# Narrower waits for index scores and the first attention pair, and later turns of finished rows, in a two-block transformer kernel

## The chip, the core and the metric

The kernel runs on one core of one Trainium2 chip. The metric is the device time of one execution in microseconds. The change is judged by the medians of several runs of each kernel. TensorE (PE) multiplies matrices and turns (transposes) tiles into PSUM, VectorE (DVE) and ScalarE (ACT) read PSUM and write SBUF, GpSimd (POOL) and SyncE (SP) issue DMAs. Each engine works through its own list in order and waits on semaphores.

## The reference

Two blocks of two layers each work on 512 rows of width 1024, all in float32.

```python
# first block, each layer
h = x @ w_in                     # split in diff_q/k/v, dsa_q/k/v, idx_q/k/w, fox_q/k/v/f, gate
a  = rms(diff_attention(rope(dq), rope(dk), dv, lam)) * g_subln     # 4 heads
bo = dsa_attention(...)          # keys chosen by index scores, top 128
co = forgetting_attention(...)   # 4 heads
x  = layer_norm(ALPHA * x + (concat(a, bo, co) * silu(gate)) @ w_out)
# the choice of keys in dsa_attention
sc = einsum('bqhd,bsd->bqhs', qi, ki)
idx_score = einsum('bqhs,bqh->bqs', relu(sc), wi)
_, idx = top_k(where(causal, idx_score, -inf), topk)

# second block, each layer (256 context rows beside the 512)
q, k, v = split(modulate(rmsnorm(x)) @ w_qkv)    # 16 query heads, 4 key heads of 64
o = window_attention(...)        # layer 0, with a sink per head
o = global_attention(...)        # layer 1, with normed queries and keys
x = x + gate_a * (o @ w_o)
x = x + gate_f * moe(modulate(rmsnorm(x)))       # 32 experts, 2 for each row
return rmsnorm(x)
```

## The kernel before

`make_plan` writes out one list of steps, and every engine walks through the same list in `build`, each doing its share of a step. The order of the steps is therefore the order of each engine's work. Rows are in tiles of 128 (`t`). Three rings carry the work between the engines: the two banks of `PJ` (projections and weighed values), the two banks of `TR` (turned tiles), the two halves of `SC` (scores). A use number counts up for each ring (`n["tr"]` for TR). TensorE waits before use k of TR until use k-2 was copied out (`tr_slot`, `tr_free`), and ScalarE copies each turned bank to SBUF and then adds one to `tr_free`.

First block. For each chunk of w_in (`idx_q`, `idx_k`, `dsa`, `fox`, `diff_q`, `diff_k`, `diff_v`, `gate0`, `gate1`) and each tile there is a `project` step (L1120 to L1129), then `flush(1)`, which issues the `stage_turn` (L1136) of the tile before: TensorE turns what VectorE rotated into STG, and ScalarE copies it to QK. In the three chunks dsa, fox and diff_q (`ci` 2, 3, 4) an `index` step follows (L1155): scores of one pair of index heads for the query tile `ci - 1`, which ScalarE passes through relu and VectorE weighs and sums. Further `topk` steps of VectorE go through the summed scores. TensorE waits in an index step until `tr_free` has reached `s.tr_before`, the number of all TR uses planned up to there. The step reads blocks 8 to 11 (idx_q) and 12 (idx_k) of QK alone. In the first dsa tile a `forget` step stands between the turn and the index step.

Second block. The columns of w_qkv come in three chunks c in the order 0, 2, 1 (queries of heads 0 to 7, keys and values, queries of heads 8 to 15), with a `qkv` step (L1288) per tile and a `qk_turn` (L1302) of the tile before by `flush2(1)`. Attention runs in units, one head of one query tile each, two units per call of `attend_pair(unit_list, i, after)`. A call issues the scores of units i and i+1, the turn of i-2 (L1186), the exponential of i, the weighing of i-3 (L1196), the exponential of i+1, the turn of i-1 and the weighing of i-2. ScalarE copies each turn into PT. The first call stands before the last `qkv` step of chunk 1. Its first unit waits for `tr_free` to reach `u.needs`, again all uses planned so far. It reads keys and queries of head 0 of tile 0. In layer 1 VectorE and ScalarE do their part of that last `qkv` step only in the step `qkv_late`, after pair 2. `flush2(0)` turns this late tile after pair 4. `rq`, in layer 1, also after pair 4, takes roots and reciprocals of the query norms for heads 8 to 15. `gains`, in layer 0, after pair 8, folds gains into the rope tables on VectorE.

When the last unit k of a query tile has been weighed, VectorE divides the result into O2, and `after[k]` issues the `o_turn` step: TensorE waits for `pj_free`, turns the 1024 columns of the tile in two banks (`turn_rows`, L1081), and ScalarE copies both to XT. `attend_pair` issues it at the end of pair k+3. There are six such tiles in layer 0 (80 units) and four in layer 1 (64 units). The output projection (`wo_first`, `wo`, L1086) follows after all pairs.

Of the kernel before, what the change touches and what calls it, by code (L numbers as in the profile page):

```python
# [171 lines left out]
def make_plan(until=99):  # L172


    steps = []
    n = dict(pj=0, tr=0, sc=0, stg=0, unit=0, fin=0, bc=0, topk=0, idx=0, ada=0, mixed=0, part=0, sinks=0, routed=0)
# [3 lines left out]
    def take(what, k=1):  # L180
        n[what] += k
        return list(range(n[what] - k, n[what]))
# [14 lines left out]
    def add(kind, **kw):  # L197
        s = Step(kind=kind, tr_before=n["tr"] - len(kw.get("tr", ())), **kw)
        steps.append(s)
        users = kw.get("w")  # L200
        if users is not None and kw.get("last", True):

            for u, use in zip(users if isinstance(users, list) else [users], kw["pj"] if isinstance(kw["pj"], list) else [kw["pj"]]):
                u.done = use + 1
        return s

    def begin_unit(u, first):
        u.sc = take("sc")[0]
        u.index = attend.count
        attend.count += 1  # L210
        u.two_before = units_before[-2] if len(units_before) >= 2 else None
        units_before.append(u)
        n["mixed"] += u.kind == "diff"
        u.mixed = n["mixed"]
        u.first = first
        if u.slot == 0:
            attend.batch += 1
            n["sinks"] += u.kind in ("window", "ctx")
        u.batch, u.sinks = attend.batch, n["sinks"]
        s = add("scores", u=u)  # L220
        u.needs = s.tr_before

    def turn_unit(u):
        u.tr = take("tr", -(-u.blocks // 4))
        add("turn", u=u)
# [10 lines left out]
    def attend_pair(unit_list, i, after):  # L236


        m = len(unit_list)
        if i < m:  # L240
            begin_unit(unit_list[i], i == 0)
            begin_unit(unit_list[i + 1], False)
        if 2 <= i < m + 2:
            turn_unit(unit_list[i - 2])
        if i < m:
            add("exp", u=unit_list[i])
        if 4 <= i:
            weigh_unit(unit_list[i - 3])
        if i < m:
            add("exp", u=unit_list[i + 1])  # L250
        if 2 <= i < m + 2:
            turn_unit(unit_list[i - 1])
            weigh_unit(unit_list[i - 2])
        if i - 3 in after:
            after[i - 3]()

    def attend(unit_list, extra=None, after=None):

# [37 lines left out]
    for l in range(DEPTH):  # L296
# [29 lines left out]
        for ci, name in enumerate(names):  # L326
            w = weight("w_in", l=l, cols=CHUNKS[name])
            for t in range(XT_TILES):
                if l and ci == 0 and t == XT_TILES - 1:
                    xt_ready[t] = add("fin_turn", f=fins[t], tr=take("tr", 2)).tr[-1]  # L330
                s = project(name, t, w)
                turn_staged(s)
                flush(1)
                if name == "dsa" and t == 0:
                    add("forget", l=l, pj=take("pj")[0])
                if ci >= 2:

                    if ci - 1 in (1, 2, 3):
                        add("index", l=l, t=ci - 1, h=2 * t, sc=take("sc")[0], index=take("idx")[0])
                    for tt in (1, 2, 3):  # L340
                        if topk_left[tt] and tt < ci - 1:
                            k = min(4 if ci < 5 else 2, topk_left[tt])
                            topk_left[tt] -= k
                            add("topk", l=l, t=tt, rounds=k, last=topk_left[tt] == 0,
                                count=n["topk"] + (topk_left[tt] == 0))
                            n["topk"] += topk_left[tt] == 0
                            break
            if name == "idx_k":
                add("log_f", l=l)
# [6 lines left out]
        unit_list = []  # L356
# [47 lines left out]
    for l in range(DEPTH):  # L404
# [5 lines left out]
        def flush2(keep):  # L410
            while len(prev) > keep:
                add("qk_turn", s=(s := prev.pop(0)), tr=take("tr", s.turns))

        unit_list, last_unit = [], []
# [15 lines left out]
        def oturn(t):  # L430
            def go():
                turned[t] = add("o_turn", t=t, after=unit_list[last_unit[t]].pj, tr=take("tr", 2)).tr[-1]
            return go

        after = {k: oturn(t) for t, k in enumerate(last_unit)}
        late = None
        for p, c in enumerate((0, 2, 1)):
            w = weight("w_qkv", l=l, c=c)
            ts = list(range(XT_TILES) if (last and c < 2) else range(tiles))
            if l == 0 and c == 0:  # L440
                ts = ts[XT_TILES:] + ts[:XT_TILES]
            if l and c == 2:
                add("load2", l=l)
                add("layer2", l=l)
                add("rq", l=l, c=0)
            for t in ts:
                if p == 2 and t == ts[-1]:
                    attend_pair(unit_list, 0, after)
                if l == 0 and c == 0 and t == 0:
                    xt_ready[XT_TILES - 1] = add("fin_turn", f=fins[-1], tr=take("tr", 2)).tr[-1]  # L450
                two = c < 2 and t < XT_TILES
                ahead = combines[4 * p + t + 1] if l and 4 * p + t + 1 < len(combines) else None
                tr = take("tr", 2) if ahead else None
                s = add("qkv", l=l, c=c, t=t, w=w, last=t == ts[-1], pj=take("pj")[0], stg=take("stg", 2 if two else 1),
                        turns=2 if two else 1, inner=(ahead, tr) if ahead else None)
                if l and p == 2 and t == ts[-1]:
                    late = s
                    s.late = True
                s.ready = xt_ready[t] if (l == 0 and c == 0) or (l and (c == 0 or (c == 2 and t >= XT_TILES))) else None
                if ahead:  # L460
                    xt_ready[ahead.t] = tr[-1]
                prev.append(s)
                if l and 4 * p + t + 2 < len(combines):
                    add("combine_end", f=combines[4 * p + t + 2], l=l - 1)
                    if 4 * p + t + 3 < len(combines):
                        front(4 * p + t + 3)
                flush2(1)
        for i in range(2, len(unit_list) + 4, 2):
            attend_pair(unit_list, i, after)
            if i == 2 and late:  # L470
                add("qkv_late", s=late)
            if i == 4:
                if l:
                    add("rq", l=l, c=1)
                flush2(0)
            if i == 8 and l == 0:
                add("gains", l=l)
# [23 lines left out]
        t = moe_tiles - 1  # L501
# [2356 lines left out]
```

How the kernel before makes its waits and increments, by code:

```python
        def w_ready(eng, u):  # L971
            eng.wait_ge(w_loaded[u.slot], 16 * (u.loads))
# [9 lines left out]
        @block.sync  # L982
# [2 lines left out]
            def free(prev):  # L985
                if prev is not None:
                    sp.wait_ge(sc_full if units[prev].kind in ("gate", "up") else pj_full, units[prev].done)
# [26 lines left out]
            n = 0  # L1015
            while n < len(units):
                u = units[n]
                if u.kind not in ("gate", "up", "down"):
                    load_unit(u)
                    n += 1
                    continue
                m = units[n:n + 3 * EXPERTS]
                base, l = n, u.l
                sp.wait_ge(pj_full, attended[l])
                for k in range(8):
                    free(m[k].prev)
                    load_expert(m[k], m[k].e)
                with sp.Fori(0, 14) as i:
                    for k in range(8, 14):
                        sp.wait_ge(pj_full if m[k].kind == "down" else sc_full,
                                   i * (4 if m[k].kind == "down" else 2) + m[k - 6].done)
                        load_expert(m[k], i * 2 + m[k].e)
                for k in range(92, 96):
# [4 lines left out]
                    for u in units[n:n + 3]:  # L1039
                        load_unit(u)
                    n += 3
                o = over[l]
                sp.wait_ge(over_ready, l + 1)
                sp.wait_ge(pj_full, m[-1].done)
                count = sp.value_load(OVI[0:1, MAX_OVER:MAX_OVER + 1], min_val=0, max_val=MAX_OVER)
```

## Time and profile before

| | us |
|---|---|
| runs, median of 3 | 2954.38 (2951.1 to 2954.95) |
| profiled execution, whole | 2950.66 |
| its span in the profile | 2949.0 |
| TensorE busy | 2803.7 (95%) |
| VectorE busy | 1144.1 (39%) |
| ScalarE busy | 761.1 (26%) |
| GpSimd busy | 323.3 (11%) |

The span goes roughly as follows: projections of the first layer to 285 us, its attention to 400, the second layer of the first block from 460 to 850 with the same stages, projections of the second block to 1070, window attention to 1243, experts from about 1360 to 1940, the last layer's projections to 2080, its attention to 2253, experts again to the end. Times in a timeline are microseconds from the span's start. A row of it gives start and duration of one or more merged instructions, the engine, the line of the kernel, the operation with its tiles and shape, and their number. A bracket gives the idle time of the engine ahead of it and who ended that. All VectorE and ScalarE work is recorded under L140. A matmul of float32 counts as several instructions.

### The profile page before, as it was taken

Reading aid. Unit: us, or ns where it says so; the run is one execution under the profiler, and the core shown is the slowest. Engines: PE = TensorE matmul, PEld = TensorE weight load, DVE = VectorE, ACT = ScalarE, POOL = GpSimd, SP = SyncE. Lnnn points to the kernel's source line nnn. Section 1 sums busy time; section 2 is a strip of 40 time slices with the busy share of each in tenths; the row PEclk is TensorE's granted clock in tenths of the full one; section 3 lists DMA queues with packets and bytes.
Section 4 is the critical chain, followed back from the end, with each engine's and each line's share of the span. In section 5 each row is a group of like instructions: output and inputs, shape, how many; then the busy total and the mean of one; then the engine's idle time right before and its main releaser. Section 6 shows DMA issues by size and latency. Waiting matters only on the chain. (4 is left out here: it accounts for less than half of the span.)

```text
span 2949.0 us, 65190 instructions
## 1 busy us (share of the span) xinstructions
PE 2803.7 (95%) x27105; PEld 1659.6 (56%) x27109; DVE 1144.1 (39%) x2781; ACT 761.1 (26%) x1599; POOL 323.3 (11%) x584
## 2 busy tenths in 40 slices
PE   8999999999889999999999999989899999999996
PEld 4444655444554457645666666644576566666663
DVE  2572653472654245545211122253443611112214
ACT  1111531110542147621111111143674111111111
POOL 3000430000440000011010000020000100000011
PEclk9999999999989999999999999999999999999998
DMA  7212653211653100146999999962002599999994
GB/s 272 70 57 86 231 161 97 78 66 57 238 186 137 57 1 2 57 166 222 397 401 400 397 398 401 396 235 99 1 2 108 210 384 400 399 399 401 399 400 169
DMA packets 155504, 636.94 MB, mean 216 GB/s; under 512 B 19744, under 2 KB 24352, under 8 KB 138960
## 3 DMA queue, kind: packets, MB, share of 16 engines
q1 hardware_dynamic: 114624, 517.59, 45.5%
q0 software_dynamic: 40720, 117.18, 11.7%
q8 instruction: 106, 1.74, 0.2%
q14 instruction: 54, 0.44, 0.0%
HBM read 582.70 MB, written 52.00 MB: 215 GB/s over the span
## 5 line engine op out<-in xcount | busy, mean ns | idle before, releaser
L1128 PE MATMUL PJ<-WR,XT 128*128 128x512 f32 (+2 forms) x1152 | 475.2, 568 | 5.7 <-ACT XT L140 2.9
L140 ACT ACTIVATE PT<-TR 128x512 f32<-128x512 f32 (+3 forms) x384 | 177.8, 493 | 880.6 <-PE TR L1357 736.9
L1128 PEld LDWEIGHTS PJ<-WR,XT 128*128 128x128 f32 x1152 | 215.6, 191 | 243.9 <-issue 215.7
L140 DVE TENSOR_TENSOR PR<-G 128x384 f32<-128x384 f32 x64 | 35.8, 559 | 737.9 <-ACT G L140 737.5
L1086 PE MATMUL PJ<-WR,XT 128*128 128x512 f32 x576 | 260.1, 608 | 1.8 <-ACT XT L140 1.4
L1337 PE MATMUL SC<-QK,XT 128*64 128x256 f32 x2112 | 244.1, 385 | 0.0
L140 DVE TENSOR_REDUCE SM<-SC 128x1 f32<-128x768 f32 (+6 forms) x208 | 173.7, 835 | 152.6 <-PE SC L1106 143.8
L1288 PE MATMUL PJ<-WR,XT 128*128 128x512 f32 x512 | 227.1, 596 | 1.0 <-issue 1.0
L1337 PE MATMUL SC<-WR,XT 128*64 128x256 f32 x1984 | 226.2, 381 | 0.0
L1337 PEld LDWEIGHTS SC<-QK,XT 128*64 128x64 f32 x2112 | 150.2, 138 | 86.3 <-issue 16.0
L140 ACT ACTIVATE PR<-SC,SM 128x256 f32<-128x256 f32 (+5 forms) x288 | 187.6, 669 | 41.4 <-DVE SM L140 27.2
L140 ACT ACTIVATE XT<-TR 128x384 f32<-128x384 f32 (+1 forms) x204 | 99.6, 526 | 343.8 <-PE TR L1323 241.6
L1086 PEld LDWEIGHTS PJ<-WR,XT 128*128 128x128 f32 x576 | 110.2, 195 | 133.5 <-issue 131.3
L1337 PEld LDWEIGHTS SC<-WR,XT 128*64 128x64 f32 x1984 | 139.8, 137 | 79.6 <-issue 12.3
L1196 PE MATMUL PJ<-V,PT 128*64 128x65 f32 (+1 forms) x3904 | 169.0, 233 | 1.4 <-ACT PT L140 1.4
L1106 PE MATMUL SC<-QK 64*128 64x512 f32 (+7 forms) x512 | 157.5, 522 | 10.8 <-ACT PR L140 10.6
L1186 PE MATMUL TR<-KF,PR 128*128 128x128 f32 x976 | 149.2, 282 | 10.0 <-DVE PR L140 7.4
L1196 PEld LDWEIGHTS PJ<-V,PT 128*64 128x64 f32 x3904 | 136.8, 138 | 36.4 <-issue 33.4
L1288 PEld LDWEIGHTS PJ<-WR,XT 128*128 128x128 f32 x512 | 95.2, 191 | 109.1 <-issue 109.1
L140 ACT ACTIVATE QK<-TR 128x512 f32<-128x512 f32 (+4 forms) x108 | 59.2, 563 | 369.7 <-PE TR L1136 272.6
L2765 POOL DMA_DIRECT2D y_rows<-XT x62 | 33.2, 535 | 950.1 <-DVE XT L140 925.2
L1347 PE MATMUL SC<-QK,XT 128*32 128x128 f32 x4224 | 127.9, 273 | 0.0
(253 smaller groups left out, 3344.0 us busy)
## 6 DMA issues: line engine op xcount, KB each, us to landing
QK<-in_w_gate_dram SPq DMA_DIRECT2D x34, 2048.0 KB, 9.5
WR<-in_w_down_dram SPq DMA_DIRECT2D x34, 2048.0 KB, 15.8
QK<-in_w_up_dram SPq DMA_DIRECT2D x32, 2048.0 KB, 14.4
WR<-in_w_up_dram SPq DMA_DIRECT2D x32, 2048.0 KB, 14.4
WR<-in_w_gate_dram SPq DMA_DIRECT2D x30, 2048.0 KB, 9.5
QK<-in_w_down_dram SPq DMA_DIRECT2D x30, 2048.0 KB, 15.9
WR<-in_w_ada_dram SPq DMA_DIRECT2D x24, 2048.0 KB, 8.1
WR<-in_w_in_dram SPq DMA_DIRECT2D x14, 2048.0 KB, 7.9
```

What stands on the lines that cost most here:

```text
L140: return lambda *a, **k: Signal(make(*a, **k), self)
L1086: m = mm(dst[:, 0:n], rows[:, c, :], w[:, c, 0:n], start=c == 0, stop=c == DC - 1)
L1106: m = mm(SC[:, u.sc % 2, col:col + n], lhsT, rhs, start=all(p[0] // 512 != bank for p in ps[:k]), stop=all(p[0] // 512 != bank for p in ps ...
L1128: m = mm(bank[:, 0:n], XT1[:, c, s.t * P:(s.t + 1) * P], w[:, c, 0:n], start=c == 0, stop=c == DC - 1)
L1186: m = turn(bank[:, b * P:(b + 1) * P], src, identF)
L1196: m = mm(bank[r:r + HALF_ROWS, col:col + n], PT[:, o + r:o + r + HALF_ROWS], v, start=b == 0, stop=b == len(vs) - 1)
L1288: m = mm(bank, rows[:, c, :], w[:, c, :], start=c == 0, stop=c == DC - 1)
L1337: mm(bank[CAP_A * h:CAP_A * (h + 1), k * 512:k * 512 + 256], XET[par][:, c, 0:CAP_A], w[:, c, 256 * h:256 * (h + 1)], start=c == 0, stop=c ...
L1347: x = mm(bank[CAP_B * q:CAP_B * (q + 1), k * 512 + 256:k * 512 + 384], XET[par][:, c, CAP_A:CAP], w[:, c, P * q:P * (q + 1)], start=c == 0 ...
L2765: dma(dst, YR[r % 2][0:CAP]).then_inc(y_stored[r % 2], 16)
```

## The change

In `attend_pair` the call of `after` moves: from the end of pair k+3 to the middle of pair k+5, between the exponential of unit i and the weighing of unit i-3. The weighing of i-3 gets an upper bound, since the loop now runs one pair further (the last pair holds only the last `o_turn`). In the first block the index steps get `indices_turned` as the value that they wait for, taken at the first dsa tile ahead of the first index step. In the second block the first unit gets `keys_turned`, taken after the turns behind the first tile of chunk 1. `flush2(0)` moves from pair 4 to pair 8, in both layers, and stands before `gains` in layer 0; `rq` stays.

```diff
@@ attend_pair
         if i < m:
             add("exp", u=unit_list[i])
-        if 4 <= i:
+        if i - 5 in after:
+            after[i - 5]()
+        if 4 <= i < m + 4:
             weigh_unit(unit_list[i - 3])
         if i < m:
             add("exp", u=unit_list[i + 1])
         if 2 <= i < m + 2:
             turn_unit(unit_list[i - 1])
             weigh_unit(unit_list[i - 2])
-        if i - 3 in after:
-            after[i - 3]()
@@ make_plan, first block
                 if ci >= 2:
 
+                    if ci == 2 and t == 0:
+                        indices_turned = n["tr"]
                     if ci - 1 in (1, 2, 3):
                         add("index", l=l, t=ci - 1, h=2 * t, sc=take("sc")[0], index=take("idx")[0])
+                        steps[-1].tr_before = indices_turned
@@ make_plan, second block
                 if p == 2 and t == ts[-1]:
                     attend_pair(unit_list, 0, after)
+                    unit_list[0].needs = keys_turned
@@
                 flush2(1)
-        for i in range(2, len(unit_list) + 4, 2):
+                if p == 2 and t == ts[0]:
+                    keys_turned = n["tr"]
+        for i in range(2, len(unit_list) + 6, 2):
             attend_pair(unit_list, i, after)
             if i == 2 and late:
                 add("qkv_late", s=late)
             if i == 4:
                 if l:
                     add("rq", l=l, c=1)
+            if i == 8:
                 flush2(0)
             if i == 8 and l == 0:
                 add("gains", l=l)
```

## Rows read from the trace of the kernel before

**Rows 1.** The page's busy times: engine, busy us (share of the span), instructions.

```profile
PE 2803.7 (95%) x27105; PEld 1659.6 (56%) x27109; DVE 1144.1 (39%) x2781; ACT 761.1 (26%) x1599; POOL 323.3 (11%) x584
```

**Rows 2.** TensorE's waits: line, releaser: us in total, times, longest.

```profile
PE TR L1081 <- DVE G L140: 25.3, 15, 5.2
PE SC L1155 <- ACT QK L140: 17.5, 22, 1.0
```

**Rows 3.** TensorE's timeline, turn and index in a dsa, a fox, a diff_q step.

```profile
82.60 0.49 PE L1136 MATMUL TR<-KF,STG 128*128 128x128 f32 x3
83.75 0.70 PE L1155 MATMUL SC<-QK 64*128 64x256 f32 x4 [0.66 <-ACT QK L140]
...
114.43 1.04 PE L1136 MATMUL TR<-KF,STG 128*66 128x128 f32 x8
116.41 0.92 PE L1155 MATMUL SC<-QK 64*128 64x384 f32 x4 [0.95 <-ACT QK L140]
...
172.66 0.60 PE L1136 MATMUL TR<-KF,STG 128*128 128x128 f32 x4
174.03 1.13 PE L1155 MATMUL SC<-QK 64*128 64x512 f32 x4 [0.77 <-ACT QK L140]
```

**Rows 4.** TensorE's timeline, a turn and scores that don't wait, layer 1, second block.

```profile
2079.13 1.04 PE L1302 MATMUL TR<-KF,STG 128*128 128x128 f32 x8
2080.10 0.48 PE L1106 MATMUL SC<-V,QK 64*128 64x256 f32 x1
```

**Rows 5.** Stretches: us, busy PE, PEld, DVE, ACT, POOL; clock, DMA share, GB/s.

```profile
83.75:106.61 22.86, 20.87 (x70) 10.95 (x70) 9.73 (x38) 3.26 (x6) 0.00 (x0) 1.00 0.27 92
145.83:183.00 37.17, 34.86 (x98) 15.38 (x99) 31.53 (x71) 6.11 (x8) 0.00 (x0) 1.00 0.16 57
1400.00:1600.00 200.00, 200.00 (x2829) 126.75 (x2823) 42.85 (x83) 23.73 (x55) 19.25 (x35) 1.00 1.01 399
```

**Rows 6.** VectorE's timeline, the index sum in a diff_q step.

```profile
176.41 1.54 DVE L140 SCALAR_TENSOR_TENSOR BC<-PT,SM,BC 128x512 f32<-128x512 f32 x2 [0.68 <-ACT PT L140]
```

**Rows 7.** TensorE's timeline, turn and first pair's scores, layers 0 and 1.

```profile
1059.66 1.04 PE L1302 MATMUL TR<-KF,STG 128*128 128x128 f32 x8
1061.51 0.48 PE L1106 MATMUL SC<-V,QK 64*128 64x256 f32 x1 [0.82 <-ACT QK L140]
...
2067.26 1.04 PE L1302 MATMUL TR<-KF,STG 128*128 128x128 f32 x8
2070.67 0.48 PE L1106 MATMUL SC<-V,QK 64*128 64x256 f32 x1 [2.37 <-ACT QK L140]
```

**Rows 8.** Timelines of TensorE and ScalarE around the first `o_turn` of layer 0.

```profile
1105.41 0.80 PE L1196 MATMUL PJ<-V,PT 128*64 128x65 f32 x20
1107.37 1.06 PE L1081 MATMUL TR<-KF,G 128*128 128x128 f32 x8 [1.16 <-ACT PT L140]
1108.36 0.48 PE L1106 MATMUL SC<-V,QK 64*128 64x256 f32 x1
...
1106.63 0.77 ACT L140 ACTIVATE PT<-TR 128x512 f32<-128x512 f32 x2
```

**Rows 9.** Timelines of TensorE, ScalarE, VectorE around layer 1's late turn.

```profile
2089.03 0.92 PE L1196 MATMUL PJ<-V,PT 128*64 128x65 f32 x24
2094.68 1.94 PE L1302 MATMUL TR<-KF,STG 128*128 128x128 f32 x8 [4.73 <-ACT PT L140]
...
2109.17 0.48 PE L1106 MATMUL SC<-V,QK 64*128 64x256 f32 x1
...
2092.92 0.99 ACT L140 ACTIVATE PR<-SC,SM 128x768 f32<-128x768 f32 x1 [0.28 <-DVE SM L140]
2094.88 1.28 ACT L140 ACT_TABLE_LOAD   x1
...
2096.91 0.18 DVE L140 TENSOR_SCALAR SM<-SM 128x32 f32<-128x32 f32 x1
```

**Rows 10.** The stretch behind the late turn, columns as in Rows 5.

```profile
2092.00:2102.00 10.00, 7.32 (x52) 5.44 (x52) 3.84 (x10) 6.66 (x11) 0.00 (x0) 0.66 0.00 0
```

## The prediction

> **What bounds the kernel now.** I read the page's busy times first: TensorE is busy for 95% of the span [rows 1]. A microsecond is won where TensorE stands still and nothing else takes the place of the wait, and nowhere else. So the second view is the list of what TensorE waited for, and in it two of the largest entries: 25.3 us of transposes (L1081) behind VectorE's G, and 17.5 us of index scores (L1155) behind ScalarE's QK, 22 waits [rows 2]. The source splits the first: L1081 is shared by every transpose of whole rows, and much of the 25.3 belongs to steps that the change leaves alone (its longest, 5.2 us, stands behind the sub-norm). The second is touched by the change in full. The rest is read instruction by instruction in the timeline of TensorE, ScalarE and VectorE around each touched place, always as start against start, since the "idle" of a row leaves out the tail of a matmul whose end is modelled.
>
> **Index scores.** The wait of `index` on `tr_free` asks for all turns so far, and so for the copy of the turn issued just ahead of it. With the new value it asks only for the turns of idx_q and idx_k, which were over before the first index step. Per layer there are 12 index steps; the first is already covered by `forget`, 11 wait. What stands between turn and index now, start to start: 1.15 us behind a turn of three blocks, 1.98 behind one of eight, 1.37 behind one of four [rows 3]. What would stand there without a wait: a turn of eight with scores of 64 rows behind it that don't wait takes 0.97 [rows 4]; eight blocks last 1.04 and four 0.60 [rows 3], 0.11 for each block, so 0.53 for four and 0.42 for three. The gain is then 0.73, 1.01 and 0.84 each. Per layer four follow a three-block turn (dsa, and the first fox step), four an eight-block turn (three fox steps and the first diff_q step), three a four-block turn: 2.9 + 4.0 + 2.5 = 9.5, twice 18.9 us. The lower end is the idle time that the waits show, 17.5 [rows 2]; the upper end counts no 0.1 for the change from 128 to 64 rows, 22 x 0.1 more, 21.1.
>
> Who would be late next? Behind the index stands the next projection, which needs a PJ bank that VectorE freed a period ago. ScalarE's relu comes after the copy in its order, and that copy is done by then or shortly after. VectorE is the engine to look at: in the diff_q steps it does the rotation, the index sum and four rounds of top-k, and is busy 31.53 of 37.17 us [rows 5]. In a step of 9.4 us (165 to 174) it stands idle for 0.68 only, behind the relu [rows 6], so it needs 8.7 us where TensorE would want 8.56. It falls behind by 0.15 us per step for three steps, and TensorE's turn of a staged tile comes a whole projection after VectorE wrote it, some six microseconds of slack. In the dsa steps it is busy for 9.73 of 22.86 [rows 5]. After diff_q two rounds stand in place of four and it catches up. I charge nothing.
>
> **First pair of the second block's attention.** Its scores now ask for all turns so far; with `needs` set after the last key turn they ask for nothing that is late. Layer 0: from turn to scores 1.85 us [rows 7], 0.97 without a wait, gain 0.9. Layer 1: 3.41 [rows 7], gain 2.4, since there the copy stands behind the staging copy and the square of the next tile on ScalarE. The exponentials of that pair come no earlier (VectorE takes their minima after its rotation), but TensorE has a projection before it needs them, and the next turn starts only at 2079.13 [rows 4]. In layer 1 ScalarE would end the second exponential just as the next turn is ready, so this cover is thin; without it up to 1 us goes. Sum 3.3, from 2.3 to 3.5.
>
> **Finished rows turned a pair later.** Ten `o_turn` steps; the last of each layer stays behind the last weighing, eight move. Before: the weighing starts at 1105.41 and lasts 0.80, the turn waits 1.16, the next scores start at 1108.36 [rows 8], so the step costs 2.15. The wait is for ScalarE: its copy of the preceding turn, at 1106.63, stands behind the pair's second exponential [rows 8]. Moved between `exp` and `weigh` of the following pair, the turn comes right behind the turn of unit i-2. Its rows have long been written by VectorE. The bank it needs is freed by a copy that ScalarE can start at once: bank full after 0.6, copy 0.6 (the pair of copies lasts 0.77 for five blocks [rows 8]), where TensorE would be there after 0.55, so it waits 0.7; with its own 0.9 that is 1.6. Queued behind it now are a weighing and the turn of unit i-1; its two copies, about 1.1 us (an estimate from 0.77 for five blocks), stand on ScalarE ahead of the pair's second exponential, and the turn of i-1 waits perhaps 0.1 for a bank. The pair after finds both exponentials done. Where a unit has four blocks one bank is already free and the wait is 0.4, but before it was shorter too. I take 2.15 + 0.1 - 1.6 = 0.7 for each, 5.6 for eight. Ends: nothing gained (each new wait as long as the old), and 8 x 1.2 = 9.6 with no wait left.
>
> **The late query tile.** Layer 1: the weighing at 2089.03 is done at 2089.9, and the turn of the late tile waits 4.73 us for a bank whose copy stands behind the exponential of unit 5; it starts at 2094.68 [rows 9]. The granted clock is 0.66 over the ten microseconds from 2092 [rows 10], so 6.8 of them at 1.2 GHz, and the turn lasts 1.94 instead of 1.04. The scores of pair 10 (units 10 and 11) start at 2109.17 [rows 9]. Without the turn there, the next scores wait for the two exponentials (unit 5's ends at 2093.91 [rows 9]) and start at about 2092.7. This wait of 2.8 us takes the place of the 4.8. Then comes the root of the query norms: its table load at 2094.88 takes 1.28 [rows 9], VectorE is held until 2097.1 [rows 9], takes the minima of units 6 and 7, and the exponentials, 0.99 each [rows 9], follow another table load, so that they end at about 2100.5 and 2101.5. Pair 8 then starts at about 2100.6, when the first of them has freed its scores, and takes 4.9, pair 10 without more would start at 2105.5. The late turn is now behind pair 8, in the position that `o_turn` leaves, and costs about 2.0 there: 2107.5 against 2109.17, gain 1.7. Should the clock fall here as well, the waits for VectorE absorb most of it (0.3). Ends: -1 (the root's chain a little later than I have it) and +5. Layer 0: the turn finds its bank free in both places; one pair before the `gains` step it covers some 0.5 us of waits behind it. Sum 2.2.
>
> The Trainium skill, "ScalarE: Activation LUTs", section "Table sets: the hidden batching unit", says to batch activations by set and prices a switch at about 2.7 us. That speaks against leaving the root between exponentials; by its price two loads would set pair 8 back by 2.8 us and the late tile would cost 1.1 instead of giving 1.7. The rows show 1.28 for a load in this kernel, and the measured value decides.
>
> **Sum.** 18.9 + 3.3 + 5.6 + 2.2 = 30.0 us. No instruction is added or removed, no DMA is moved, and the queues of SP and POOL keep their order.
>
> **Rivals.**
> (a) The moved turns give nothing, because ScalarE, loaded with two more copies inside a pair, makes the second exponential late: only the first two parts remain, 22.2. For it: two exponentials of 0.99 and two units' copies of at least 0.77 [rows 8, 9] keep ScalarE for over 3.5 us of a pair of some 4.9 already. Against it: the pair that follows has slack. 2928.5 by the profiled run.
> (b) The index waits turn into waits for VectorE or a bank and only the other parts count, 11.1: 2939.6. For it: the 0.68 us in [rows 6]. Against it: it concerns three steps a layer, and the lag is far from TensorE's need.
> (c) The gain is given back in the expert stage, whose DMA share is 1.01 from 1400 to 1600 [rows 5]: if the stream of weights began at a fixed time, TensorE would only wait for it, and the total would be unchanged, 2950.7. Against it: SP's loads wait for the last weighing and for consumed slots, so they move with TensorE.
> (d) Slower. The turns inside a pair leave short waits in a row (bank, weighing, bank) at eight places, and the clock falls to 1.2 GHz at each for 6.8 us as at 2092 [rows 10], which costs 3.4 us. With waits that long the moved turns give nothing either, so the base is that of (a): ten falls (eight turns, the two late tiles) are 34 against 22.2, 2962.5. [...]
> The Trainium skill, "TensorE: Matmul & The Clock Gate", section "A second HAM failure mode: psum-queue depth-cycling", says that frequent micro-idles between groups of matmuls make the clock oscillate. By that rule (d) is what eight new micro-idles do; the stretches of index steps, with one such idle each period, don't show it.
>
> **How the numbers follow.** The profiled execution took 2950.7 us (span 2949.0); less 30.0 that is 2920.7. The median of the runs before is 2954.4, 3.7 higher, and the profiled one lies below all three, so I add half of that: 2922.5. Chances: my forecast 0.82, (a) 0.08, (b) 0.05, (c) 0.03, (d) 0.02. The ends of the unknown parts: 17.5 + 2.3 + 0 - 1 = 18.8 and 21.1 + 3.5 + 9.6 + 5.5 = 39.7, which gives 2911 to 2932 by the profiled run; with the 3.7 of the median at the upper end, and (a) inside, 2911 to 2935. Of this kernel a measurement can tell about 0.2%, 6 us. Faster by more: forecast, (a) and (b), with a little off for what I didn't see, 0.94; within 0.2%: 0.04; slower: 0.02.
>
> **What would show it.** Right: no L1155 row with a wait in TensorE's list, index scores about 0.5 us behind a four-block turn and about 1.0 behind eight; first scores of the pairs 1.0 us behind their turn; `o_turn` inside a pair with a wait of 0.4 to 0.7 behind ScalarE's PT; layer 1's late turn behind pair 8, and between 2085 and 2105 no single wait over 3 us. Wrong: waits of a projection or a staged turn behind VectorE in the diff_q steps, scores waiting for the second exponential behind each `o_turn`, or new stretches of a granted clock of 0.5.

## The result, and the profile after

The changed kernel took 2923.79 us in the median (2922.1 to 2926.34, 4 runs), the kernel before 2952.74 beside it on the same chip (2945.94 to 2954.95, 4 runs). The ratio is 0.9906, with an interval of 0.989 to 0.9922: 29 us, or 0.94%, faster. The profiled execution took 2925.03 us with a span of 2923.3, so against the profiled one of before the span is 25.7 us shorter. The forecast was a median of 2922.5 us, and 30.0 us less than before in the profiled execution. The time was met, but the sum was 3 to 4 us higher than what the traces show. The parts below show where.

The page of the changed kernel, its busy times, and then TensorE's list of waits (line, releaser: us in total, times, longest). All lines of the helpers have moved down by 7: the index scores are L1162, the turns of whole rows L1088, the scores of a pair L1113, the late turn L1309.

```profile
PE 2798.9 (96%) x27109; PEld 1659.0 (57%) x27109; DVE 1143.9 (39%) x2781; ACT 760.9 (26%) x1599; POOL 323.9 (11%) x584
```

```profile
PE TR L1088 <- DVE G L140: 24.2, 14, 5.2
PE SC L1113 <- ACT PR L140: 15.5, 10, 2.7
...
PE TR L1088 <- ACT PT L140: 4.4, 8, 0.8
...
PE SC L1103 <- ACT XT L1740: 3.6, 1, 3.6
...
PE TR L1309 <- ACT PT L140: 1.1, 1, 1.1
```

Against [rows 1] the work is the same; what changed is idle time. The index scores (17.5 us in [rows 2]) have left the list. The 25.3 us behind VectorE's G have become 24.2, so that entry had, as supposed, little to do with the change. The scores behind ScalarE's PR have grown from 11.5 us in 9 waits to 15.5 in 10. The same entry in the list of before:

```profile
PE SC L1106 <- ACT PR L140: 11.5, 9, 2.5
```

It grew in layer 1, where waits of 2.74 and 1.28 us took the place of the late turn's 4.7; they are shown with the last experiment.

**Index scores.** TensorE's timeline of the changed kernel in the same diff_q step as in [rows 3]:

```profile
159.72 6.17 PE L1135 MATMUL PJ<-WR,XT 128*128 128x512 f32 x14
165.72 0.60 PE L1143 MATMUL TR<-KF,STG 128*128 128x128 f32 x4
166.25 1.13 PE L1162 MATMUL SC<-QK 64*128 64x512 f32 x4
167.31 1.13 PE L1135 MATMUL PJ<-WR,XT 128*128 128x512 f32 x2
```

Turn to scores is 0.53 us here, 1.37 in [rows 3]. From the first index step to the last a layer takes 87.79 us (78.46 to 166.25) where it took 97.32 (76.71 to 174.03), in both layers: 9.53 each, 19.06 together. Nothing turned up behind it: no projection or turn waits for VectorE in these stretches.

**The whole span, as a running account.** The same instruction is looked up in both traces, and the difference of its starts shows what has been won up to there.

| up to | before | after | won so far | part |
|---|---|---|---|---|
| first index step, layer 0 | 76.71 | 78.46 | -1.75 | start-up |
| last index step, layer 0 | 174.03 | 166.25 | 7.78 | index 9.53 |
| last index step, layer 1 | 624.00 | 606.34 | 17.66 | index 9.53 |
| output stage of layer 1 | 946.96 | 928.62 | 18.34 | small waits |
| weighing behind the first pair | 1072.72 | 1053.49 | 19.23 | first pair 0.89 |
| turn of unit 18 | 1103.27 | 1083.63 | 19.64 | late tile 0.41 |
| last row turn, layer 0 | 1243.50 | 1221.94 | 21.56 | five moved turns 1.92 |
| second block, layer 1, before its first pair | | | 22.42 | select, experts |
| behind that pair | 2084.73 | 2059.87 | 24.86 | first pair 2.4 |
| pair 10, layer 1 | 2109.17 | 2083.51 | 25.66 | late tile 0.80 |
| last row turn, layer 1 | 2252.87 | 2226.12 | 26.75 | three moved turns 1.09 |
| end of the span | 2949.0 | 2923.3 | 25.7 | experts |

So the change gave 19.06 + 3.3 + 3.0 + 1.2 = 26.6 us in these two executions. The start-up cost 1.75, and the stretches that the change doesn't touch moved both ways, by up to 1.6 us at one place (the wait of L1103 in the list above is 3.6 us here and 2.0 in the same place before). Such stretches vary from trace to trace. From the last row turn of layer 1 to the end of the span, where no edit lies, five traces take 694.7 to 697.2 us (before and changed among them) and the seven others 700.7 to 701.5, and a second trace of the changed kernel is one of those. The medians of the kernel before differ in the same way from chip to chip, 2948.84 to 2954.26 us. A part of a few microseconds is therefore read inside its own stretch and not from the whole span.

### The profile page after: what moved, and what is told of

It is laid out like the page before. It is cut to its first block and busy times, and to the rows that moved or that the text cites. A ratio compares the mean times of both kernels' runs of the same rounds, so it can differ in the third digit from the quotient of the medians.

```text
span 2923.3 us, 65195 instructions
## 1 busy us (share of the span) xinstructions
PE 2798.9 (96%) x27109; PEld 1659.0 (57%) x27109; DVE 1143.9 (39%) x2781; ACT 760.9 (26%) x1599; POOL 323.9 (11%) x584
## 5 line engine op out<-in xcount | busy, mean ns | idle before, releaser
L1113 PE MATMUL SC<-QK 64*128 64x512 f32 (+7 forms) x512 | 157.7, 522 | 11.1 <-ACT PR L140 11.0
```

Source lines behind the costliest of these rows:

```text
L1113: m = mm(SC[:, u.sc % 2, col:col + n], lhsT, rhs, start=all(p[0] // 512 != bank for p in ps[:k]), stop=all(p[0] // 512 != bank for p in ps ...
```

## The experiments

Each is one kernel, read in the same way; where several executions were timed, the median, the range and the ratio to the kernel before on the same chip stand with it.

### The index scores alone

```diff
 (kernel before)
+                    if ci == 2 and t == 0:
+                        indices_turned = n["tr"]
 ...
+                        steps[-1].tr_before = indices_turned
```

> The kernel before with nothing but the index steps' new value for their wait. My theory: the index waits alone carry 19 of the gain, since TensorE bounds the projection steps and nothing is late behind them: about 19 us faster than before (0.64%), first to last index step 9.5 us shorter in each layer, and no wait of a projection or a staged turn behind VectorE. Rival (VectorE or a bank becomes the bound in the diff_q steps): 14 us or less. Rival (the gain needs the other parts, because it is given back at a later wait): under 10 us.

Measured: 2936.97 us (2933.17 to 2940.16) against 2953.16, ratio 0.9941 [0.9924, 0.9957], 16.2 us. In its trace the stretch from the first to the last index step is 87.79 us in both layers, to the hundredth what it is in the changed kernel. The interval, 12.7 to 22.4 us, alone would still allow the rival's 14; the stretch decides for 19. The waits that belong to the other parts are all still there: in TensorE's list of this kernel the turn of the late tile waits 4.7 us and the row turns 7.3 (4.7 and 7.2 in the kernel before).

```profile
PE TR L1084 <- ACT PT L140: 7.3, 7, 1.2
PE TR L1305 <- ACT PT L140: 4.7, 1, 4.7
```

### All but the index scores

```diff
 (changed kernel)
-                    if ci == 2 and t == 0:
-                        indices_turned = n["tr"]
 ...
-                        steps[-1].tr_before = indices_turned
```

> The changed kernel with the index steps waiting as before. If the parts add up, this is faster than before by the rest of the gain, 7 to 8 us (3.3 from the first pairs, 3 from the moved rows, 1.2 from the late tile by the trace of the changed kernel; by the prediction it was 11). If the trace's account misses something outside the touched stretches, this and the index-only kernel don't add up to the whole, 27 to 29 us.

Measured: 2946.59 us (2941.31 to 2950.92) against 2953.16, ratio 0.9979 [0.997, 0.9989], 6.6 us; the parts read from the traces say 7.5. The two halves add up to 22.8 us, and the whole change gave 29.0; the intervals of the two, 0.43 to 0.76% and 0.11 to 0.30%, allow 16 to 31 us. The medians don't contradict a plain sum, though so wide a range doesn't prove one.

This trace held something that no edit explains. Behind `forget` (matmuls of four columns) the clock fell, which it had not in the profiled execution of the kernel before. TensorE's timeline and the stretch (us, busy PE, PEld, DVE, ACT, POOL; clock, DMA share, GB/s):

```profile
76.26 2.37 PE L1150 MATMUL PJ<-SM,KF 128*128 128x4 f32 x20
78.55 1.05 PE L1159 MATMUL SC<-QK 64*128 64x256 f32 x4
79.53 6.73 PE L1132 MATMUL PJ<-WR,XT 128*128 128x384 f32 x16
86.10 0.49 PE L1140 MATMUL TR<-KF,STG 128*128 128x128 f32 x3
87.25 0.70 PE L1159 MATMUL SC<-QK 64*128 64x256 f32 x4 [0.66 <-ACT QK L140]
...
78.00:82.00 4.00, 4.00 (x14) 2.38 (x14) 1.48 (x6) 0.60 (x1) 0.00 (x0) 0.60 0.03 7
```

The granted clock is 0.60 in these four microseconds, the projection takes 6.73 us where it took 5.43 in the trace of before, and layer 0's stretch of index steps is 98.97 us for 97.32: 1.65 more. Whether the old or the new wait decides that is taken up below, with the last kernels.

### The moved row turns alone, and the late tile alone

```diff
 (kernel before; first kernel)
+        if i - 5 in after:
+            after[i - 5]()
-        if 4 <= i:
+        if 4 <= i < m + 4:
 ...
-        if i - 3 in after:
-            after[i - 3]()
 ...
 (kernel before; second kernel, the line before moved from i == 4)
+            if i == 8:
                 flush2(0)
```

> The kernel before with only the finished rows' turns moved. By the trace of the changed kernel each moved turn still waits 0.75 (five blocks), 0.64 (six) or 0.33 (four) for ScalarE's copy and lengthens its pair by about 1.8 instead of 2.2: about 0.4 for each of eight, window attention 1.9 and global attention 1.1 us shorter between the first and the last turn of rows. By the prediction 0.7 each, 5.6 in all. The two can be told apart in the trace alone, not in the time.

> The kernel before with only the late tile's turn moved from pair 4 to pair 8. By the changed kernel: pair 10 of layer 1 starts 0.8 us earlier against the first pair, layer 0 gains 0.4, and behind pair 4 a wait of 2.7 for the exponential of unit 4 takes the place of the 4.7. Rival (what the changed kernel shows there is the work of the moved rows or of the first pair): pair 10 no earlier than before.

Measured, one execution each: 2949.47 and 2949.48 us. Beside runs of before that spread from 2947.16 to 2958.09 that says nothing, so the stretches are compared. Window attention (weighing behind the first pair to the last row turn) takes 170.78 us in before, 168.87 with the row turns alone and 170.67 with the late tile alone: 1.91 for five turns, and 0.11 for the late tile. The late tile did win its 0.40 us (37.81 us for 38.21 from the scores of the second call to the scores behind the first row turn), but a later pair, which its edit doesn't touch, took 4.66 us for 4.38; more on that below. In layer 1 (second turn of pair 2 to the last row turn) it is 169.76, 168.55 and 168.92: 1.2 for the row turns, of which 0.17 lies in pair 6, ahead of the first of them, and 0.84 for the late tile. So each part alone is what it is in the changed kernel: 3.0 for the row turns, and 0.40 and 0.84 for the late tile. Row turns moved inside the pair are worth 0.4 us each and not 0.7.

### The row turn ahead of the turn of unit i-2

Why only 0.4? The changed kernel around its first row turn of layer 0, TensorE's timeline and ScalarE's:

```profile
1088.01 0.71 PE L1193 MATMUL TR<-KF,PR 128*128 128x128 f32 x5
1089.48 1.06 PE L1088 MATMUL TR<-KF,G 128*128 128x128 f32 x8 [0.75 <-ACT PT L140]
1090.47 0.80 PE L1203 MATMUL PJ<-V,PT 128*64 128x65 f32 x20
1091.21 0.76 PE L1193 MATMUL TR<-KF,PR 128*128 128x128 f32 x5
```

```profile
1088.74 0.77 ACT L140 ACTIVATE PT<-TR 128x512 f32<-128x512 f32 x2 [0.99 <-PE TR L1193]
1089.54 0.80 ACT L140 ACTIVATE PR<-SC,SM 128x640 f32<-128x640 f32 x1
1090.36 1.09 ACT L140 ACTIVATE XT<-TR 128x512 f32<-128x512 f32 x2
1092.09 0.79 ACT L140 ACTIVATE PR<-SC,SM 128x640 f32<-128x640 f32 x1 [0.64 <-PE TR L1193]
```

ScalarE is free: it idles 0.99 us ahead of the copy. The turn starts at 1088.01, its copy at 1088.74 (0.73 later), and TensorE goes on at 1089.48 (1.47 later). That is the trip of a bank from TensorE to ScalarE and back, and no queue is in it. If it is the cause, the wait must go when the row turn stands ahead of the turn of i-2, where both banks are long free.

```diff
 (changed kernel, attend_pair)
+        if i - 5 in after:
+            after[i - 5]()
         if 2 <= i < m + 2:
             turn_unit(unit_list[i - 2])
 ...
-        if i - 5 in after:
-            after[i - 5]()
```

> The changed kernel with each turn of finished rows issued one place earlier in its pair: behind the two scores and ahead of the turn of unit i-2. Theory: the wait that is left in the changed kernel (0.75, 0.64, 0.33) stands there only because the turn of rows follows another turn, whose bank ScalarE has yet to copy. Ahead of it both banks are free, the wait of the row turn is 0, the turn of unit i-2 waits about 0.3 for a bank in its place, and a pair with a row turn is longer by about 1.3 instead of 1.8: 3 to 4 us less than the changed kernel over eight turns. Rival: ScalarE's two additional copies, not the bank, set the length of the pair; then the wait only moves to the turn of i-2 or to the scores behind and the time stays the changed kernel's.

Measured: 2919.24 us (2917.77 to 2920.65) against 2948.84, ratio 0.9898 [0.9874, 0.9921]. TensorE's timeline:

```profile
1086.20 0.40 PE L1113 MATMUL SC<-KB 128*128 128x128 bf16 x4
1086.44 1.04 PE L1088 MATMUL TR<-KF,G 128*128 128x128 f32 x8
1087.90 0.74 PE L1193 MATMUL TR<-KF,PR 128*128 128x128 f32 x5 [0.42 <-ACT XT L140]
```

The row turn waits for nothing, and the turn of i-2 waits 0.42 us for a bank in its place. A moved row turn can change the pair behind it too: with four blocks that pair takes 3.50 us in the changed kernel, where it takes 3.86 here. So the table gives the pair with the row turn and the pair behind it together, from start of scores to start of scores:

| two pairs, the first with a row turn | before | changed | ahead | without a turn |
|---|---|---|---|---|
| five blocks | 10.98 | 10.51 | 10.25 | 8.76 |
| six blocks (layer 1) | 11.85 | 11.41, once 11.69 | 11.19 | 9.70 |
| four and five blocks | 9.08 | 8.78 | 8.70 | |
| four blocks | 9.43 | 9.13, once 9.40 | 9.19 | 7.70 |

For five blocks a row turn costs 2.22 us before, 1.75 changed and 1.49 ahead, for six 2.15, 1.71 and 1.49, for four 1.73, 1.43 and 1.49. The order ahead is therefore worth 0.27, 0.22 and, with four blocks, nothing: 1.2 us over eight turns beside the changed kernel, where 3 to 4 were expected. The medians can't show it: 29.6 us less than before here, 29.0 for the changed kernel on another chip. That the row turn's wait goes when both banks are free agrees with the trip of the bank. But with four blocks the wait only moves to the turn of i-2 and the time stays, as the rival said, so what sets the length of those pairs is open.

The two turns that took 0.27 us more in the changed kernel (at 1192 and 2192) are not an effect of the turn. In the pair that holds it the second of two exponentials starts 0.36 us behind the end of the first, and TensorE's second scores wait for it. ScalarE, then TensorE, changed kernel:

```profile
1190.44 0.84 ACT L140 ACTIVATE PR<-SC,SM 128x256 f32<-128x256 f32 x2 [0.36 <-ACT PR L140]
...
1191.33 0.70 PE L1113 MATMUL SC<-V,QK 64*128 64x256 f32 x4 [0.38 <-ACT PR L140]
```

Both stand at the same places in the second trace of the changed kernel. Other kernels have the like in pairs without a row turn: 4.39 us for 4.13 in before, behind a pause of 0.39, and 4.66 for 4.38 with the row turns alone, with the late tile alone and here, where a copy of ScalarE starts 1.00 us behind its turn and not 0.72. What holds ScalarE there is open. In layer 0 the changed kernel has lost one and gained one, so its account isn't changed by them; in layer 1 it has gained one, and without it the three turns there would have given about 1.3 instead of 1.09.

In layer 1 this trace wins nothing of that (168.43 us for 167.88). The clock didn't fall in pair 6 behind the wait of 2.74, as it does in the changed kernel, but in pair 8, behind one of 1.65, where a turn of six blocks takes 1.54 us for 0.87. Pair 8 starts as before, 17.63 us behind the second turn of pair 2 for 17.64, but from there to the late turn it is 8.12 us for 6.64, 1.5 more.

### The late tile ahead as well

```diff
 (the kernel before this one)
-            attend_pair(unit_list, i, after)
+            attend_pair(unit_list, i, after, (lambda: flush2(0)) if i == 10 else None)
 ...
-            if i == 8:
-                flush2(0)
```

> As the one before, and the late query tile is turned in the same place of pair 10 instead of behind pair 8. If the bank explains the 1.14 us that the late turn waits in layer 1, this gives another 0.8 to 1.0 us there (layer 0 has no such wait and gains nothing): about 4 to 5 us less than the changed kernel in all, 31 to 33 less than before.

Measured: 2919.36 us (2916.74 to 2925.57) against the same 2948.84, ratio 0.9900 [0.9881, 0.992], which is 29.5 us where 31 to 33 were expected, and no difference from the kernel before it in the medians. In the trace the late turn is in pair 10 without a wait and costs 1.49 us, for 2.20 behind pair 8; layer 1 takes 166.25 us for 167.88. In layer 0 nothing is won, as expected: window attention takes 168.88 us, for 168.22 in the kernel before this one, and two pairs that take 4.07 us for 3.72, one close behind pair 10 and one far from it, make up that difference.

```profile
2081.43 1.09 PE L1309 MATMUL TR<-KF,STG 128*128 128x128 f32 x8
...
2082.95 0.84 PE L1193 MATMUL TR<-KF,PR 128*128 128x128 f32 x6 [0.42 <-ACT QK L140]
```

### How thick VectorE's cover of the index scores is

```diff
 (changed kernel)
-                            k = min(4 if ci < 5 else 2, topk_left[tt])
+                            k = min(8 if ci == 4 else 4 if ci < 5 else 2, topk_left[tt])
```

> The changed kernel with eight rounds of top-k in place of four in the first two diff_q steps and none in the next two: the same work of VectorE, crowded. It measures the cover that the index gain rests on. Eight rounds make a step of VectorE about 13.7 us against TensorE's 8.56. If the staged turns have some 6 us of slack, TensorE waits behind VectorE by about 10.3 - 6, 3 to 5 us per layer, in all at the turns of the first diff_q tiles. If the cover is larger than I think, there is no wait; if it were thin (a rival's premise), TensorE would wait close to 10 us per layer.

Measured, one execution: 2944.99 us. TensorE's timeline, then the stretch around it:

```profile
159.75 6.17 PE L1135 MATMUL PJ<-WR,XT 128*128 128x512 f32 x14
170.65 1.11 PE L1143 MATMUL TR<-KF,STG 128*128 128x128 f32 x4 [4.73 <-DVE STG L140]
171.69 2.08 PE L1162 MATMUL SC<-QK 64*128 64x512 f32 x4
...
165.00:185.00 20.00, 15.27 (x38) 6.67 (x37) 13.43 (x27) 2.22 (x3) 0.00 (x0) 0.83 0.31 105
```

With eight rounds of top-k in a diff_q step for four, the turn of the staged tile waits 4.73 us in layer 0 and 4.72 in layer 1, within the 3 to 5 expected, and the clock falls behind it (scores of 1.13 us take 2.08). The stretch of index steps is 94.80 us for 87.79, but not all of the 7.0 is VectorE's. Between the first two index steps stand 7.93 us for 6.32, since the clock fell behind `forget`, as it did in some of the other traces too. The last step takes 13.96 us for 8.56, which is 5.4 for the wait and the low clock, and from the last scores to the next turn of a staged tile it is 10.03 for 8.03, 2.0 more by the low clock. So rival (b) is a real mechanism, and the changed kernel is on the near side of it: with four rounds nothing waits, with eight some 7.4 of the 9.5 us that a layer's index steps give are lost again.

### The order that both readings favour, beside the changed kernel

```diff
 (changed kernel: row turns ahead as above, and)
+            attend_pair(unit_list, i, after, (lambda: flush2(0)) if l and i == 10 else None)
 ...
-            if i == 8:
+            if i == 8 and l == 0:
                 flush2(0)
```

> The version that the two runs before point to: turns of finished rows ahead of the turn of unit i-2, and layer 1's late tile in the same place of pair 10, while layer 0's late tile stays behind pair 8. From their traces: 2.6 us over eight row turns and 0.7 for the late turn, 3.3 us less than the changed kernel, which runs on the same chip in the same call. Rival: what the turns give is taken back by other waits, and the two are the same in time. With some 4 us between single runs of one kernel, the medians may not separate them.

> The changed kernel itself, on the same chip as the version above, in five rounds: 26 to 29 us less than before. The trace's account of the touched stretches gives 26.6; what the medians show beyond that would lie outside them.

Measured on one chip, against 2954.26 for the kernel before: 2924.73 us (2921.99 to 2928.01), ratio 0.9898 [0.988, 0.9916], and 2926.55 (2920.98 to 2927.85), ratio 0.9901 [0.9885, 0.9917], for the changed kernel. In the traces the new order is 0.23 us shorter in window attention (168.26 for 168.49) and 1.59 in layer 1 (166.28 for 167.87): 1.8 in all, of which 1.16 is the row turns' and 0.67 the late tile's. The expected 3.3 had 2.6 for the row turns, which comes from comparing only the pairs that hold them and leaves out the pair behind each. The medians differ by 1.8 us too, but the ranges lie over each other: an order that is better in the trace, by an amount that the times can't confirm.

The start-up and the clock behind `forget` can now be laid out over the profiled executions. These are the stretches 24 to 32 us and 78 to 82 us (columns as above) of the changed kernel, of the same kernel again, and of the last one:

```profile
24.00:32.00 8.00, 5.47 (x11) 2.44 (x12) 2.16 (x5) 2.34 (x4) 8.00 (x16) 0.79 1.05 404
78.00:82.00 4.00, 4.00 (x18) 2.57 (x18) 1.43 (x5) 0.60 (x1) 0.00 (x0) 1.00 0.02 4
```

```profile
24.00:32.00 8.00, 5.48 (x11) 2.44 (x12) 2.16 (x5) 2.34 (x4) 8.00 (x16) 0.79 1.05 402
78.00:82.00 4.00, 4.00 (x13) 2.38 (x14) 1.43 (x5) 0.60 (x1) 0.00 (x0) 0.57 0.02 5
```

```profile
24.00:32.00 8.00, 5.63 (x20) 3.02 (x20) 2.08 (x5) 3.34 (x6) 8.00 (x16) 1.00 1.04 403
78.00:82.00 4.00, 4.00 (x10) 2.13 (x9) 0.84 (x2) 0.25 (x1) 0.00 (x0) 0.68 0.00 0
```

The changed kernel has a clock of 1.00 behind `forget` in one execution and 0.57 in the other. So neither kind of wait decides that. At the start, kernels of both kinds stand on both sides too. The first index step comes at 78.45 to 78.55 with the index part alone, with all but it, with the late tile alone and in both traces of the changed kernel, and at 76.6 to 76.9 in before and the other six. The granted clock between 24 and 32 us is 0.79 in each of the first five traces and 1.00 in each of the seven others.

### Without the root of the query norms

```diff
 (changed kernel, rq)
+                    if s.c == 1:
+                        A(by_half(RQ, s.c), by_half(SSQ, s.c), ACT.Identity, ...)
+                    else:
                         A(by_half(RQ, s.c), by_half(SSQ, s.c), ACT.Sqrt, ...)
```

> The changed kernel with the square root of the query norms of heads 8 to 15 in layer 1 replaced by a plain scaling, which leaves that root out of what is computed: the same instruction count, but ScalarE needs no table load for it and none back to the exponential. The prediction put the start of pair 8 down to this chain. Theory: with both loads (2.56 us) gone the wait of 1.28 ahead of pair 8 and the 0.5 inside it go, pair 8 starts about 1.3 us earlier against the start of pair 2, pair 10 about 1.8 earlier. Rival (the late tile's rotation on VectorE sets the start of pair 8 too): less than 0.5 us.

What this bears on, first in the changed kernel, layer 1. TensorE's waits between pair 2 and pair 10, and ScalarE beside them:

```profile
2058.24 0.85 PE L1193 MATMUL TR<-KF,PR 128*128 128x128 f32 x6 [0.64 <-ACT PT L140]
2067.82 0.69 PE L1113 MATMUL SC<-V,QK 64*128 64x256 f32 x1 [2.74 <-ACT PR L140]
2075.88 0.48 PE L1113 MATMUL SC<-V,QK 64*128 64x256 f32 x1 [1.28 <-ACT PR L140]
2082.52 1.06 PE L1309 MATMUL TR<-KF,STG 128*128 128x128 f32 x8 [1.14 <-ACT PT L140]
```

```profile
2070.01 1.28 ACT L140 ACT_TABLE_LOAD   x1
...
2073.54 1.28 ACT L140 ACT_TABLE_LOAD   x1 [0.68 <-issue]
2074.83 2.06 ACT L140 ACTIVATE PR<-SC,SM 128x768 f32<-128x768 f32 x2
```

Measured without the root, one execution: 2927.18 us. The table loads are gone, and so is the wait of 1.28:

```profile
2056.90 0.84 PE L1193 MATMUL TR<-KF,PR 128*128 128x128 f32 x6 [0.64 <-ACT PT L140]
...
2074.34 0.48 PE L1113 MATMUL SC<-V,QK 64*128 64x256 f32 x1
...
2080.35 1.06 PE L1309 MATMUL TR<-KF,STG 128*128 128x128 f32 x8 [1.14 <-ACT PT L140]
...
2064.00:2076.00 12.00, 9.52 (x78) 6.28 (x79) 6.18 (x14) 6.90 (x11) 0.00 (x0) 0.72 0.00 0
```

Pair 8 starts 17.44 us behind the second turn of pair 2 (17.64 in the changed kernel), the late turn at 23.45 for 24.28. So taking the root and its two loads away gives 0.2 us at pair 8, where 1.3 were expected, and 0.8 at the late turn. The 0.2 is in the rival's range, but the late tile's rotation isn't what holds pair 8: TensorE works without a wait from 2066.48 to 2074.34. What holds it is the clock, 0.72 between 2064 and 2076: most of pair 6, behind the wait of 2.74, runs at the lower level, and the pair takes 7.86 us, for 4.85 of a pair at full clock. In the changed kernel it takes 8.06 (2067.82 to 2075.88), with the root's chain in it and a shorter fall (0.86 over the same twelve microseconds). In the kernel with the row turns ahead the clock stays at 1.00 there, the root's chain is in it, and pair 8 starts at 17.63. So the slow clock and the root's chain lie beside each other, and either alone fills the three microseconds.

## Why the prediction was right, and where it was off

**What bounds the kernel** held: time was won where TensorE stood idle, with the work of every engine unchanged, and the experiment with more top-k rounds is the only one that made another engine the bound.

**Index scores**: forecast 18.9, measured 19.06. The three prices of turn to scores came out as they were taken: 0.53 behind four blocks, 0.42 behind three (84.36 to 84.78), 0.96 behind eight (113.26 to 114.22). That VectorE is not late next was argued from slack and is now bracketed: no wait at four rounds, 4.73 us at eight.

**First pairs**: forecast 0.9 and 2.4, measured 0.89 and 2.4. The cover that was called thin in layer 1 held: the next turn had its bank.

**Moved row turns**: forecast 0.7 each and 5.6 in all, measured 0.4 and 3.0. Place and mechanism were right; what failed is the sum "2.15 + 0.1 - 1.6 = 0.7". Its 0.1 is the wait that the moved turn brings to the turn of i-1, so it belongs with the 1.6. With the sign right the same terms give 0.45 each and 3.6 in all, beside a measured 0.47 with five blocks, 0.44 with six and 0.30 with four. So 2.0 of the missing 2.6 us are a slip of arithmetic. The terms were each a little off, and nearly cancel: the turn and its wait add 1.81 us for the 1.6 (1.47 from the turn of i-2 to the row turn, 0.99 for the row turn, less the 0.65 that lie between the turn and the weighing anyway). The turn of i-1 comes 0.08 sooner behind the weighing and not 0.1 later, and the old place cost 2.22, not 2.15, since the scores behind a weighing start 0.73 after it. The copy starts 0.73 behind the turn of five blocks, where 0.6 was taken. The waits, 0.75, 0.64 and 0.33, lie in or next to the forecast 0.4 to 0.7, so the waits alone would not have shown the slip. With the right sign the whole forecast would have been 28.0 us and not 30.0.

**Late tile**: forecast 2.2, measured 1.2 (0.41 and 0.80), again a size. Layer 1: the wait of 2.74 for the exponential (forecast 2.8) and the start of pair 8 (2100.74 by the clock of before, forecast 2100.6) came out. Pair 8 took 5.4 us, for 4.9: its second scores wait for the exponential of unit 7, which the root's chain had also delayed. The late turn cost 2.2, for 2.0, the same trip of the bank as above. That is the 0.9 between pair 10 forecast at 2107.5 and measured at 2108.37. A fall of the clock in pair 6 was to be absorbed, and it was: the start of pair 8 is the same with it (17.64) and without (17.63).

The Trainium skill, "ScalarE: Activation LUTs", section "Table sets: the hidden batching unit", gives about 2.7 us for a switch. The same page, section "What ACT_TABLE_LOAD costs", makes that up of a load of 1283 ns and a drain of about 1380 ns. The trace agrees on the load, 1.28 us each, and not on the drain: from the end of the copy at 2069.95 to the start of the root at 2071.31 it takes 1.36 us, with the load in it. Pair 8 stood where the load's duration alone puts it.

**Rivals.** (a), nothing from the moved turns because ScalarE is loaded: ruled out, it idles 0.99 ahead of the copy, and the turns give 1.9 + 1.0 us by themselves. (b): ruled out at this size of top-k. (c), given back in the expert stage: 22.03 us were won when the first expert stage began and 22.42 ahead of the next layer's first pair, so the stage moved with TensorE. (d), falling clock at the moved turns: the granted clock is 1.00 from 1070 to 1250 us and from 2080 to 2260, where all eight moved turns lie; the one fall in layer 1 stands behind a wait of 2.74 us, as that at 2092 did behind one of 4.73. The Trainium skill, "TensorE: Matmul & The Clock Gate", section "A second HAM failure mode: psum-queue depth-cycling", says that frequent micro-idles make the clock oscillate. The trace doesn't agree for this kernel: there are eight new ones of 0.33 to 0.75 us, and the clock stays at 1.00.

**The time**: the sum was 3.4 us too high by the parts (2.0 of it the sign, 1.0 the late tile), and the start-up and other untouched stretches cost 0.9 more in this execution. That the median was met to 1.3 us is partly luck: half of the distance between the profiled execution and the median had been added, 1.8 us, and the medians of the kernel before differ by more than that between the sets of runs (2948.84 to 2954.26).

## What to carry to other kernels

A wait that asks for the count of everything issued so far is worth reading against what the instruction reads: here a smaller number in 24 index steps, with no work removed, gave 19 of the 26.6 us. A turn that has to come between two others costs a full trip of the bank, TensorE to ScalarE and back, even where ScalarE is idle, so look first for a place where both banks have long been free; here that won another 0.2 to 0.3 us for each turn of five or six blocks, and nothing for those of four. When a step moves, compare the pair behind it too: the pair that holds it can lose what the next one gains. Where two delays lie beside each other (a table load chain and a fallen clock), taking one away gives little, and the trace of the kernel without it shows that.

## What the runs showed of the hardware

- The trip of a bank: a turn of five blocks to ScalarE's copy 0.73 us, start to start, and to the next turn that needs the bank 1.47, with ScalarE idle.
- The granted clock behind 20 matmuls of four columns was 1.00 in one execution and 0.57 in another of the same kernel; where it fell, the stretch of index steps was 1.6 us longer. Seventy microseconds into the span, the traces stand 1.8 us apart, five with a granted clock of 0.79 between 24 and 32 us and seven with 1.00, whatever the edit was.
- ScalarE paused 0.36 to 0.39 us between two exponentials at places that depend on the kernel, and a pair took 0.26 to 0.28 us longer by it. In two traces of one kernel the pauses stood at the same pairs.
- A wait of 2.74 us was followed by a lower clock in the changed kernel, and in another kernel it stayed at 1.00 behind the same wait. Behind `forget` it fell in some traces with no wait ahead of it.
- A pair mostly at the lower clock took 3.0 us more where nothing lay beside it, 1.5 in pair 8 of the kernel with the row turns ahead, and nothing where ScalarE's chain was longer.
